# Which running sum takes in a norm's last tiles, and where the raw low parts stand in VectorE's order

## The reference

```
for l in range(DEPTH):                                     # DEPTH = 2, ALPHA = 4 ** 0.25
    x = layer_norm(ALPHA * x + 0.5 * swiglu(x, ffn1_w_in[l], ffn1_w_out[l]), ln1_g[l], ln1_b[l])   # norm 0
    x = layer_norm(ALPHA * x + hybrid_mixer(x, ...), ln2_g[l], ln2_b[l])                           # norm 1
    x = layer_norm(ALPHA * x + memory_cross_attn(x, mem, ...), ln3_g[l], ln3_b[l])                 # norm 2
    x = layer_norm(ALPHA * x + 0.5 * swiglu(x, ffn2_w_in[l], ffn2_w_out[l]), ln4_g[l], ln4_b[l])   # norm 3

def layer_norm(x, g, b):
    mu = mean(x, axis=-1); var = mean(square(x - mu), axis=-1)
    return (x - mu) * rsqrt(var + EPS) * g + b
```

## Time and profile before

| what | value |
|---|---|
| median of three runs | 2177.24 us (2176.24 to 2179.05) |
| the profiled execution | 2176.02 us, span of its records 2174.2 us |
| granted TensorE clock | 0.998 |
| busy: PE, DVE, POOL, ACT | 99%, 52%, 48%, 37% of the span |
| the chain that ended last | PE 92%, DVE 3%, ACT 2% |
| second half of norm 0, layers 0 and 1 | around 370 and 1448 us |
| second half of norm 2, layers 0 and 1 | around 721 and 1799 us |
| second half of norm 3, layer 0 | around 1084 us |

### The profile page before, as it was taken

One profiled execution on the slowest core, in us unless ns is written; L12 is line 12 of the kernel. 1 busy time (PEld: TensorE's weight loads), 2 busy tenths in 40 slices (PEclk: granted clock), 3 DMA queues, 4 the chain that ended last, 5 costly groups with the idle time before them and its releaser, 6 DMA issues.

```text
span 2174.2 us, 26976 instructions
## 1 busy us (share of the span) xinstructions
PE 2154.5 (99%) x11032; PEld 1809.7 (83%) x11032; DVE 1131.6 (52%) x1291; ACT 804.2 (37%) x1127; POOL 1035.5 (48%) x449
## 2 busy tenths in 40 slices
PE   9999999999999999999999999999999999999997
PEld 7888889788888988888888888897787888888886
DVE  3333335987856733333453333369878476333334
ACT  3222224836444522222353222257364344222222
POOL 4444444545563644444364444445266536444443
PEclk9999999999999999999999999999999999999999
DMA  5333322333332233332233333224244223333321
GB/s 183 97 97 97 117 94 72 88 99 106 116 97 64 90 97 98 96 116 94 76 97 107 97 98 109 94 68 97 88 117 126 78 68 88 98 97 97 116 94 52
DMA packets 96044, 210.92 MB, mean 97 GB/s; under 512 B 39344, under 2 KB 52016, under 8 KB 95664
## 3 DMA queue, kind: packets, MB, share of 16 engines
q1 hardware_dynamic: 94944, 208.19, 31.4%
q10 hardware_dynamic: 976, 1.00, 0.1%
HBM read 207.06 MB, written 2.10 MB: 96 GB/s over the span
## 4 chain that ended last, share of the span: by engine, by line
PE 92%; DVE 3%; ACT 2%; DVEq 1%; POOL 1%; issue 0%; DMA 0%; ACTq 0%; SPq 0%
PE psum L700 25%; PE psum L694 25%; PE psum L697 25%; PE psum L712 2%; DVE work L1863 1%; PE psum L852 1%; PE psum L794 1%; PE psum L937 1%; PE psum L936 1%; PE psum L799 1%; PE psum L796 1%; PE psum L718 1%; PE psum L942 1%; PE psum L669 1%; POOL w_lo L587 1%; PE psum L670 1%
## 5 line engine op out<-in xcount | busy, mean ns | idle before, releaser
L587 POOL TENSOR_TENSOR w_lo<-raw,w_hi 128x1024 fp32r<-128x1024 f32 (+2 forms) x358 | 931.6, 2604 | 1110.8 <-ACT w_hi L1342 1088.9
L1342 ACT ACTIVATE w_hi<-raw 128x1024 fp32r<-128x1024 f32 (+2 forms) x358 | 401.5, 1122 | 1211.4 <-PE psum L700 1135.1
L694 PE MATMUL psum<-acts_hi,w_hi 128*128 128x512 f32 x1720 | 674.7, 392 | 0.0
L697 PE MATMUL psum<-acts_lo,w_hi 128*128 128x512 f32 x1720 | 670.1, 390 | 0.0
L700 PE MATMUL psum<-acts_hi,w_lo 128*128 128x512 f32 x1720 | 424.8, 389 | 0.0
L694 PEld LDWEIGHTS psum<-acts_hi,w_hi 128*128 128x128 f32 x1720 | 323.0, 188 | 70.6 <-issue 3.9
L697 PEld LDWEIGHTS psum<-acts_lo,w_hi 128*128 128x128 f32 x1720 | 323.1, 188 | 68.6 <-issue 2.4
L700 PEld LDWEIGHTS psum<-acts_hi,w_lo 128*128 128x128 f32 x1720 | 323.0, 188 | 66.8
L2030 DVE TENSOR_TENSOR work<-work,psum 128x512 f32<-128x512 f32 x85 | 58.4, 688 | 552.0 <-PE psum L700 552.0
L694 PE MATMUL psum<-h_hi,w_hi 128*128 128x512 f32 x616 | 239.8, 389 | 0.0
L697 PE MATMUL psum<-h_lo,w_hi 128*128 128x512 f32 x616 | 239.8, 389 | 0.0
(11 more groups left out here) (326 smaller groups left out, 2532.3 us busy)
## 6 DMA issues: line engine op xcount, KB each, us to landing
raw<-w_in SPq DMA_DIRECT2D x176, 512.0 KB, 3.6
raw<-w_out SPq DMA_DIRECT2D x64, 704.0 KB, 4.0
raw<-w_kv SPq DMA_DIRECT2D x32, 512.0 KB, 3.6
raw<-w_mix SPq DMA_DIRECT2D x26, 512.0 KB, 3.6
raw<-w_q SPq DMA_DIRECT2D x16, 512.0 KB, 3.9
raw<-w_o SPq DMA_DIRECT2D x16, 512.0 KB, 3.5
raw<-w_v SPq DMA_DIRECT2D x4, 768.0 KB, 4.2
raw<-w_mix SPq DMA_DIRECT2D x24, 128.0 KB, 3.3
```

The lines of the kernel that those rows point to most:

```text
L587: nc.gpsimd.tensor_tensor(w_lo[:, n % SPLIT, 0:width], raw[:, n % RAW, 0:width], w_hi[:, n % SPLIT, 0:width].bitcast(F32), ALU.subtract).t ...
L694: nc.tensor.matmul(o, hi, b_hi, start=start and k == 0, stop=False)
L697: nc.tensor.matmul(o, hi, b_lo, start=False, stop=False)
L1342: A(w_hi[:, n % SPLIT, 0:width], raw[:, n % RAW, 0:width], ACT.Copy).then_inc(w_hi_made, 1)
```

## The change

For the norms of `later`, `residual` now adds ALPHA x of the last tiles into zsum for all columns. A new `product_summed` adds the second half's product out of PSUM into zsum behind each `half_added`, signals it, and drains. PE's `stats_first` then takes the mean of zsqsum alone, and `stats_rest` takes that of zsum, in place of that of the last tiles of x, once the last `product_summed` has signalled. The squares go as before. The count of these signals grows by the new ones (SUM_BASE, SUMS). The very last norm keeps its way. On DVE, the raw low parts of the second half move from the head of the second half to the place ahead of the scaling of the first half's last pair (pair 6).

```
-SUM_BASE, SUMS = (0, 8, 16, 24), 32
+SUM_BASE, SUMS = (0, 9, 17, 27), 36
...
 def stats_first(layer, n, h):
     pe.wait_ge(z_summed, sum_count(layer, n, WHOLE[n] - 1))
-    column_means(mean_of(n, h), [zsum], cols, True, False)
-    column_means(square_mean_of(layer, n, h), [zsqsum], cols,
-                 not BY_HALVES[n] or last_half(layer, n, h), False)
+    if last_half(layer, n, h):
+        column_means(mean_of(n, h), [zsum], cols, True, False)
+    column_means(square_mean_of(layer, n, h), [zsqsum], cols, True, False)
 def stats_rest(layer, n, h):
...
-    pe.wait_ge(z_added, z_count(layer, n, part))
-    means = column_means(mean_of(n, h), [x[:, m, :] for m in rest], cols, False,
-                         not BY_HALVES[n] or last_half(layer, n, h))
     if last_half(layer, n, h):
-        means.then_inc(last_means, 1)
+        pe.wait_ge(z_added, z_count(layer, n, part))
+        column_means(mean_of(n, h), [x[:, m, :] for m in rest], cols, False,
+                     True).then_inc(last_means, 1)
+    else:
+        pe.wait_ge(z_summed, sum_count(layer, n, 2 * KT - 1 - WHOLE[n]))
+        column_means(mean_of(n, h), [zsum], cols, False, False)
     pe.wait_ge(z_squared, z_count(layer, n, part))
...
 residual:    for m in range(min(WHOLE[n], KT - 1), KT):
-    cols = tokens_in(n, 0)
+    cols = slice(0, SEQ) if later(layer, n) else tokens_in(n, 0)
...
+def product_summed(b):
+    V.tensor_tensor(zsum[:, HALVES[1]], zsum[:, HALVES[1]], psum[:, b, HALVES[1]],
+                    ALU.add).then_inc(z_summed, 1)
+    dve.drain()
...
 norm_by_halves:
-    if later(layer, n):
+    if h == 0 and later(layer, n):
         for m in range(WHOLE[n], KT):
-            raw_lo(layer, n, m, h, HALVES[h])
+            raw_lo(layer, n, m, 0, HALVES[0])
...
             centered_pair(n, h, k)
+            if h == 0 and k == KT - 2 and later(layer, n):
+                for m in range(WHOLE[n], KT):
+                    raw_lo(layer, n, m, 1, HALVES[1])
...
 ffn, added_b:
     half_added(m, out_bank(layer, f, m, 1), HALVES[1], 2 * ALPHA)
+    if later(layer, n):
+        product_summed(out_bank(layer, f, m, 1))
...
 attention, added_b, for each of two tiles:
     half_added(m, m - KT + 2, HALVES[1], ALPHA)
+    product_summed(m - KT + 2)
```

## The result

The changed kernel takes 2181.9 us (median of 15 runs, 2180.07 to 2183.92), the kernel before 2177.24 on the same chip (15 runs, 2175.95 to 2179.13): a ratio of 1.0021, 95% interval 1.0014 to 1.0027. It is slower, by 4.7 us against a forecast of 3.9. The profiled execution took 2180.33 us with a span of 2178.5, which is 4.3 above the span before.

A forecast was written before the change was run, and what follows sets the result against it. PE, busy 99% of the span, was taken to bound the kernel. Norms 0 and 3 give -1.29, norm 2 +5.2: +3.9 us, median 2181.1 us; own range 2180.1 to 2183.2, full range 2175.8 to 2184.6.

The forecast's parts named there:

- PE's savings: Column means on PE at norms 0, 2 and 3: seven fewer at 0.43 us each, 3.0 us if PE keeps it.
- Norms 0 and 3: Three stages with one column mean fewer each; DVE's added work fits its idle time, so PE keeps 1.29 us.
- DVE at norm 2: Added sums and drains on DVE at norm 2 make everything to the last centered pair 1.01 us later.
- The port: At norm 2 DVE and POOL take turns; POOL's split shuts out the second raw low part, variance 2.85 us late.
- What PE lost: New PE wait at norm 2, from DVE's lateness less PE's room: 2.6 us per layer, +5.2 in all.
- room of 0.26: At norm 2, DVE's last low parts of the finished x end 0.26 us before PE comes to them.
- The second rival: PE keeps all it saves, -3.0 us, 2174.2; needs DVE not late at all at norm 2; chance 0.04.
- The wider running sum: L1849 takes all columns; at norm 2 DVE's chain 0 to 0.54 us later per layer, taken as 0, else +1.1.
- The first (both raw low parts ahead of the split, -1.0 to -0.4): Rival at norm 2: second raw low part starts before POOL's split; 2176.2 to 2176.8 us, chance 0.14.
- The third (the first low part late too, 1.3 more per layer): Rival at norm 2: first raw low part also behind POOL's split; +6.5 us, 2183.7, chance 0.12.
- forecast's own range: Whole kernel, main case of chance 0.70, with the wider L1849 and a microsecond either way: 2180.1 to 2183.2 us.

The follow-up runs named there:

- first experiment: The change at norms 0 and 3 alone, norm 2 keeping the old code; 2176.28 us, ratio 0.9996 to the kernel before.
- fourth experiment: The whole change, but norm 2's second-half raw low parts stand ahead of the centering of pair 6; 2177.3 us, ratio 1.0002 to the kernel before.
- last experiment but one: The whole change without product_summed's drain, norm 2's second product_summed moved behind the scaling of pair 4; 2177.22 us, ratio 0.9997 to the kernel before.
- last experiment: The whole change, but norm 2's second-half raw low parts stay at the head of the second half; 2181.45 us, ratio 1.0021 to the kernel before.

## Why the prediction was right

**PE's savings.** L852 has 74 matmuls in place of 88, and PE's starts give 0.43 for the pair that is gone ahead of the last products of norm 2 (0.67 from L852 to the next matmul before, 0.24 now) and 0.44 for the one in the rest (1.54 and 1.10). Norms 0 and 3 kept theirs: there is no wait, and from the first of the means to those in the rest PE needs 3.89 and not 4.33 us (367.54 to 371.43 at norm 0). The first experiment's time agrees.

**DVE at norm 2.** product_summed came 0.33 behind half_added (0.34 predicted) and its successor behind the drain 0.50 later, as predicted. From half_added to the last centered pair it was 3.04 against 3.03, and to the first raw low part 3.64 against 3.64.

**The port.** POOL's split came 0.22 behind the first raw low part (0.21 predicted). The pair took 3.02, as predicted (726.60 - 723.58), so that the second had about 2.6. POOL's end gives the turn-taking a number: a split of 2.41 that ends at 726.04 has run from 723.63, while the first raw low part, 0.48 long, ended at 723.79 by its record. That is again 0.16 before the recorded end. The Trainium skill, "SBUF — State Buffer", section "A bandwidth-pool intuition that's wrong (but worth ruling out)", puts the loser's start about 115 ns behind the winner's end, from a measurement of a DMA whose descriptors waited for a DVE copy. An estimate by that figure ends the split at about 726.3; the measured 726.04 decides against it for these two operations. The variance stood 7.36 behind half_added; 7.35 was predicted.

**What PE lost.** 2.6 per layer was predicted and 2.76 and 2.73 measured. ACT's sums came 1.83 later in the stage (20.86 against 19.02), 2.85 - 0.99 = 1.86 by the prediction's figures; the low parts of the finished x set the end, as predicted. By the starts of PE's instructions, what was lost sits in five places of layer 0: 0.45 at the raw pair's start, 0.60 at the last raw low part, 1.72 at ACT's sums, 0.24 at POOL's next split, 0.61 at the last low parts of the finished x. The sum is 3.62, less 0.87 saved: 2.75. The difference to 2.6 is that the last two low parts' release took some 0.07 more, and that the matmul behind these two comes 0.34 and not 0.24 after the stop: the second matmul behind a stop starts 0.22 and not 0.12 after the first (726.39 to 726.61). The same size was missed in the fourth experiment: 0.71 - 0.26 = 0.45 by the prediction's reckoning, 0.60 measured. The term that was a little too large is the room of 0.26.

One of these places was not foreseen. Before, POOL's split of the first raw weight tile and PE arrived together (POOL and PE, timelines of the kernel before):

```profile
716.68 2.40 POOL L587 TENSOR_TENSOR w_lo<-raw,w_hi 128x1024 fp32r<-128x1024 f32 x1 [7.96 <-ACT w_hi L1342]
...
719.13 0.39 PE L794 MATMUL psum<-z_hi,w_hi 128*128 128x256 f32 x1
719.35 0.28 PE L796 MATMUL psum<-z_hi,w_lo 128*128 128x256 f32 x1
```

The split ends at 719.08, PE starts at 719.13. The list of waits shows none there, but there was no room either: PE starts 0.17 and not 0.12 behind the matmul before, and its next one 0.22 behind, as after a stop. So the 0.43 saved ahead is lost at once, in the whole change and in every experiment that has norm 2's part (a row of 0.32 to 0.34 each). The second rival (PE keeps all 3.0) was excluded by this alone, even with a DVE that is not late at all. The sum did not suffer, since the loss was reckoned against PE's place before, with the saving already given up.

**The wider running sum.** 0 was taken, +1.1 the other end. PE's wait at L852 behind DVE's L1887 is 1.3 as before: 0.

**Rivals.** The first (both raw low parts ahead of the split, -1.0 to -0.4) didn't come about, but its condition was the right one. The last experiment but one made DVE 0.35 faster against the split, past the 0.18 named as deciding, and came out at -0.6. That lies in the rival's range, but partly by luck: PE's loss there is the stop at the moved sum, not the one at the last low parts that the rival counted on. The third (the first low part late too, 1.3 more per layer) is what the last experiment shows: the second low part 1.3 later with one part of POOL between, of which 0.51 reaches the end there. The predicted 2181.1 was 0.8 below the measured 2181.9, within the forecast's own range; 0.3 of this is the 0.16 and 0.13 per layer, and the rest is no more than the interval of the ratio (3.0 to 5.9 us) leaves open. The first wait of PE on ACT at the program's start, 0.7 us before and 0.9 after, is not part of the change.

## What to carry to other kernels

Work added to an engine that is busy half of the time isn't priced by its duration but by what it meets: here 1.0 us of added DVE time cost PE 2.8, because it carried one operation across the start of another engine's 2.4 us, and 0.35 us less of it, or another order of two operations, removed most of the loss. Where two engines take turns on SBUF, write both arrival times beside each other before the change and after it. Ahead of counting a saved instruction as gained, look at the next release on its path and not at the list of waits: a release that falls on the instruction's start shows no wait and leaves no room.

## What was not expected of the hardware

A wait costs PE more than its row lists: in norm 2, 0.45 against 0.34, 0.60 against 0.34, 1.72 against 1.49 and 0.61 against 0.29, by the distance of starts. The 0.60 can be followed in the rows: idle time is counted from the recorded end of the matmul before, 0.28 after its start, while the starts here are otherwise 0.12 apart. From 725.77 to 726.39 is 0.62, thus 0.50 more than 0.12; the next start, 0.22 behind, adds 0.10. And the turns of DVE and POOL were regular to some hundredths of a microsecond: the split runs from 0.16 before the recorded end of the raw low part ahead of it in the whole change, and from 0.15 before it in the kernel with the second sum later (726.14 - 2.41 = 723.73 against 723.88).
